# Where the expert bias is split into bf16 parts, how branch B normalises its rows, and the order of the first sums

## The chip, the cores and the metric

The kernel runs on one core of a Trainium2 chip. The metric is the time of one execution on the device in microseconds (us), median of several runs. One core has TensorE (PE in the profile; PEld is its weight load), VectorE (DVE), ScalarE (ACT), GpSimd (POOL) and SyncE (SP, which here only issues DMAs and waits). Every engine runs its own list of instructions in order, and they meet at semaphores.

## The reference

One decoder layer on 512 tokens of width 1024. Cut to what matters here:

```python
h = rms_norm(x, g_mix_pre) * (1.0 + sc_m) + sh_m           # sc, sh, gt: six parts of silu(c) @ w_ada + b_ada
qa, ka, va, qb, kb, vb, gza, gzb = split(h @ w_in)
o_a = sliding_window_attention(qa, ka, va, sinks, bias_a)  # branch A, 8 heads
# branch B, 4 heads with two softmaxes each, in blocks of 128 queries:
sc = jnp.einsum('bhmqd,bhmkd->bhmqk', qblk, kt)            # m = 0, 1
p = jax.nn.softmax(where(dist >= 0, sc + bias, -inf), axis=-1)
a = p[:, :, 0] - lam * p[:, :, 1]
o = einsum('bhqk,bhkd->bqhd', a, vt)
o_b = rms_norm(o, subln_g, 1e-5) * (1.0 - lam_init)
y = sigmoid(gza) * (o_a @ w_out[:512]) + sigmoid(gzb) * (o_b @ w_out[512:])
x = x + gt_m * rms_norm(y, g_mix_post)
h = rms_norm(x, g_ffn_pre) * (1.0 + sc_f) + sh_f
# 32 experts, top 4 of them for a token, blocks of 128 rows of one expert:
gu = xb @ w_gate_up[e] + b_gate_up[e]                      # up is used as clip(up) + 1
yb = clamped_swiglu(gu) @ w_down[e] + b_down[e]
```

## The kernel before

Weights and activations are fp32. In the projection and in the experts each is split into a high part (a rounding copy, on ACT) and a low part (original minus high, on DVE), and three matmuls with the parts stand for one (`three`, lines 1610 to 1612).

Stage 1, the modulation (0 to 48 us of the trace). The row silu(c) @ w_ada is made in halves of 512 contracted rows (`FIRST_MODS`, numbered 0 to 7). Halves 1, 3 and 7 are done by PE (`row_half`, L1557), the others by DVE as four multiply-adds each (`first_ada`, L1707 and L1709) whose result PE sums over partitions (`row_sum`, L1563). Between them DVE scales the four blocks of the input x (`hx`, L1736), PE transposes each (L1592) and ACT copies it out (`ht`, L1468). `hx` has two buffers, so DVE's third block waits for PE's first transposes. ACT copies finished rows (`mrow`, L1476), PE turns them to columns (`columns`, L1570), and with the last of these DVE forms the columns `shcol` and `gcol` (L1752, L1753), applies them to `ht` (L1762) and makes the high and low parts `hh` and `hl` that the projection multiplies. The first weight half of the projection is split in between: high part on ACT (L1480) after the four row copies, low part on DVE (L1745) after its first sums.

Stage 2, the projection (48 to 249 us): after K and V of branch A, eight units `u` of 512 columns (N_T = 3 transposed ones to `qk`, then five to `nat`). A unit is two weight halves, 48 matmuls each. ACT splits the second half when the unit before is done (`acc_done`), the first half of the next unit when this unit's first half is used (`half0_used`), and copies out the four sums of the unit (L1509). DVE makes the low parts and, between them, the later modulation sums (`ada`, L1724). POOL in this time issues DMAs only: small inputs, `oh` and, later, the table of position biases (`toep`), by way of DRAM.

Stage 3, attention (249 to 369 us): 24 units `UNITS`, for each block n = 0 to 3 of 128 queries two units of branch A (4 heads each) and four units of branch B (one head each, both softmaxes, keys 0 to n). PE's order is transposed(i), scores(i+3), values(i). DVE's is, in step i: after(i+1), which divides the exponentials by their sums, and before(i+3), which adds bias and takes the maximum; after the last B unit of a block `sub_norm` (L553 and L558, with a power on POOL in between, L1812). ACT's is copies(i), which brings the transposed probabilities to SBUF (L606), and exps(i+3) (L590), which also sums the rows. In steps 8 to 14 DVE does in addition one of seven `bias_parts` each (L538 to L549): they split the experts' gate and up bias `ball` (loaded three times, 32 rows each) into three bf16 parts `bparts` of 96 rows in all, which later a matmul adds to each expert's sums.

Stage 4, merge, router and tables (369 to about 480 us), and stage 5, the experts (to the end), aren't touched but for one wait of PE at their head.

For a unit of B, after(i) is four instructions: two reciprocals in one (L524), the second times minus lambda (L526), the first probabilities times the first reciprocal (L527), and the sum of both (L529).

## Time and profile before

| | |
|---|---|
| median of 3 runs | 1775.54 us (1775.3 to 1778.35) |
| the profiled execution | 1777.53 us, of which the span of the trace is 1775.7 us |
| PE busy | 1663.3 us, 94% of the span |
| DVE busy | 1377.4 us, 78% |
| ACT busy | 1097.6 us, 62% |
| POOL busy | 199.0 us, 11% |
| mean granted TensorE clock | 0.953 of full |

A share over the whole span is mostly that of the experts, which take two thirds of it; the stages before them have other limits, so the views are to be read by stage. A timeline row is: start in us, duration, engine, line, operation, output <- inputs, count of merged instructions, and in brackets the idle time before it with what ended it. The granted clock is 1.00 at 2.4 GHz and 0.50 at 1.2 GHz; a value in between is a mean over a stretch with both.

### The profile page before, as it was taken

Reading aid. Unit: us, or ns where it says so; the run is one execution under the profiler, and the core shown is the slowest. Engines: PE = TensorE matmul, PEld = TensorE weight load, DVE = VectorE, ACT = ScalarE, POOL = GpSimd, SP = SyncE. Lnnn points to the kernel's source line nnn. Section 1 sums busy time; section 2 is a strip of 40 time slices with the busy share of each in tenths; the row PEclk is TensorE's granted clock in tenths of the full one; section 3 lists DMA queues with packets and bytes.
Section 4 is the critical chain, followed back from the end, with each engine's and each line's share of the span. In section 5 each row is a group of like instructions: output and inputs, shape, how many; then the busy total and the mean of one; then the engine's idle time right before and its main releaser. Section 6 shows DMA issues by size and latency. Waiting matters only on the chain.

```text
span 1775.7 us, 19642 instructions
## 1 busy us (share of the span) xinstructions
PE 1663.3 (94%) x7482; PEld 1299.8 (73%) x7482; DVE 1377.4 (78%) x1029; ACT 1097.6 (62%) x903; POOL 199.0 (11%) x154
## 2 busy tenths in 40 slices
PE   8999986688679999999999999999999999999994
PEld 3788864444368888888888888888888888888882
DVE  3544458825558888988898889988989898989894
ACT  2322235531447777777777777777777777777772
POOL 1200000021300001100110011001000100011112
PEclk9999997888579999999999999999999999999997
DMA  8765430022499999999999999999999999999964
GB/s 310 226 236 198 168 125 1 1 77 73 140 361 398 390 385 381 367 386 382 378 355 388 383 375 366 388 392 380 361 383 387 375 370 390 380 370 361 382 244 155
DMA packets 156502, 540.14 MB, mean 304 GB/s; under 512 B 13949, under 2 KB 15081, under 8 KB 156292
## 3 DMA queue, kind: packets, MB, share of 16 engines
q1 hardware_dynamic: 140880, 500.20, 74.0%
q0 software_dynamic: 13424, 34.47, 8.0%
q10 hardware_dynamic: 2100, 4.21, 0.7%
q8 instruction: 57, 0.93, 0.2%
q14 instruction: 41, 0.33, 0.0%
HBM read 522.54 MB, written 29.26 MB: 311 GB/s over the span
## 4 chain that ended last, share of the span: by engine, by line
PE 74%; DMA 2%; DVE 2%; ACT 1%; issue 1%; POOL 0%; POOLq 0%; SPq 0%; ACTq 0%; DVEq 0%
PE ps L1103 64%; PE ps L1077 4%; PE ps L651 4%; PE ps L1093 2%; PE ps L671 1%; DMA expert_sums<-yb,icur 0%; DMA xb<-h_ffn,stab 0%; DMA sums<-expert_sums 0%; PE ps L449 0%; PE ps L664 0%; ACT h2t L755 0%; DMA slot_rows<-rows,dest 0%; DVE y L831 0%; DVE yo L1364 0%; POOL slot_rows L931 0%
## 5 line engine op out<-in xcount | busy, mean ns | idle before, releaser
L1221 DVE TENSOR_TENSOR wl<-rawm,wh 128x2048 fp32r<-128x2048 f32 x420 | 946.7, 2286 | 147.6 <-ACT wh L1150 143.1
L1150 ACT ACTIVATE wh<-rawm 128x2048 fp32r<-128x2048 f32 x420 | 802.0, 1919 | 260.7 <-PE ps L1103 260.7
L1103 PE MATMUL ps<-wh,xh 128*128 128x512 f32 x1120 | 360.2, 403 | 3.5 <-DVE xl L1234 3.5
L1103 PE MATMUL ps<-wl,xh 128*128 128x512 f32 x1120 | 346.9, 391 | 0.0
L1103 PE MATMUL ps<-wh,xl 128*128 128x512 f32 x1120 | 346.2, 390 | 0.0
L1103 PEld LDWEIGHTS ps<-wh,xh 128*128 128x128 f32 x1120 | 211.3, 189 | 53.1 <-DVE xl L1234 4.9
L1103 PEld LDWEIGHTS ps<-wl,xh 128*128 128x128 f32 x1120 | 211.2, 189 | 44.8
L1103 PEld LDWEIGHTS ps<-wh,xl 128*128 128x128 f32 x1120 | 211.3, 189 | 44.5
L1103 PE MATMUL ps<-wh,ah 128*128 128x512 f32 x560 | 179.4, 401 | 2.5 <-DVE al L1238 2.5
L1103 PE MATMUL ps<-wl,ah 128*128 128x512 f32 x560 | 174.2, 392 | 0.0
L1103 PE MATMUL ps<-wh,al 128*128 128x512 f32 x560 | 173.1, 390 | 0.0
L1306 POOL DMA_INDIRECT expert_sums<-yb,stab x32 | 50.9, 1590 | 1009.0 <-ACT yb L1184 658.1
L1103 PEld LDWEIGHTS ps<-wh,al 128*128 128x128 f32 x560 | 105.6, 189 | 23.1
L1103 PEld LDWEIGHTS ps<-wl,ah 128*128 128x128 f32 x560 | 105.5, 188 | 22.7
L1103 PEld LDWEIGHTS ps<-wh,ah 128*128 128x128 f32 x560 | 100.3, 189 | 19.6 <-issue 3.0
L1745 DVE TENSOR_TENSOR wlf<-raw,whf 128x2048 fp32r<-128x2048 f32 (+1 forms) x18 | 39.1, 2173 | 90.1 <-ACT whf L1480 90.1
L1480 ACT ACTIVATE whf<-raw 128x2048 fp32r<-128x2048 f32 (+1 forms) x18 | 32.7, 1817 | 64.2 <-PE ps L1612 64.0
L1610 PE MATMUL ps<-whf,hh 128*128 128x512 f32 (+1 forms) x192 | 71.3, 372 | 0.0
L1612 PE MATMUL ps<-whf,hl 128*128 128x512 f32 (+1 forms) x192 | 71.1, 370 | 0.0
L1611 PE MATMUL ps<-wlf,hh 128*128 128x512 f32 (+1 forms) x192 | 71.0, 370 | 0.0
L1295 POOL DMA_INDIRECT xb<-h_ffn,stab x32 | 65.4, 2043 | 47.5 <-PE ps L1077 36.1
L1176 ACT ACTIVATE ah<-ps 128x1024 fp32r<-128x1024 f32 x35 | 35.9, 1026 | 55.3 <-PE ps L1103 55.3
(254 smaller groups left out, 1610.5 us busy)
## 6 DMA issues: line engine op xcount, KB each, us to landing
rawm<-in_w_gate_up SPq DMA_DIRECT2D x280, 1024.0 KB, 9.6
rawm<-in_w_down SPq DMA_DIRECT2D x140, 1024.0 KB, 7.8
raw<-in_w_ada SPq DMA_DIRECT2D x20, 1024.0 KB, 5.1
raw<-in_w_in SPq DMA_DIRECT2D x16, 1024.0 KB, 5.2
rawx<-in_w_ada SPq DMA_DIRECT2D x4, 1024.0 KB, 15.5
wo<-in_w_out SPq DMA_DIRECT2D x2, 2048.0 KB, 15.6
bias_vectors_repeated<-bias_vectors POOLq DMA_DIRECT2D x1, 2304.0 KB, 15.6
xs<-in_x ACTq DMA_DIRECT2D x1, 2048.0 KB, 12.9
```

Of the source, the lines that this page charges most:

```text
L651: ins = nc.tensor.matmul(ps[:, 2 * b + half, :], src[:, k, t * P:(t + 1) * P], wo[:, 4 * b + k, half * UN:(half + 1) * UN], start=(k == 0) ...
L1077: ins = nc.tensor.transpose(TURNED[:, k // 4, (k % 4) * P:(k % 4 + 1) * P], src[:, k * P:(k + 1) * P], ident[:])
L1103: ins = nc.tensor.matmul(banks[:, n, :], left[:, kk, :], right[:, k, n * UN:(n + 1) * UN], start=begins and kk == 0 and i == 0, stop=kk == ...
L1150: nc.scalar.activation(flat(wh[v % SPL][:]), flat(rawm[v][:]), ACT.Copy).then_inc(wh_done, 1)
L1176: nc.scalar.activation(flat(ah[:]), flat(TURNED), ACT.Copy).then_inc(ah_done, 1)
L1221: nc.vector.tensor_tensor(flat(wl[v][:]), flat(rawm[v][:]), flat(wh[v % SPL][:]), ALU.subtract).then_inc(wl_done, 1)
L1295: pool.indirect_dma_start(out=xb[:], out_offset=None, in_=h2_d, in_offset=bass.IndirectOffsetOnAxis(ap=column(0, p, gcur, p - (E - 1)), ax ...
L1306: pool.indirect_dma_start(out=sum_d, out_offset=bass.IndirectOffsetOnAxis(ap=column(1, p, done, p - (E - 1) if done is scur else 1), axis= ...
L1610: nc.tensor.matmul(dst, a_h, b_h, start=first, stop=False)
L1611: nc.tensor.matmul(dst, a_h, b_l, start=False, stop=False)
L1612: return nc.tensor.matmul(dst, a_l, b_h, start=False, stop=last)
L1745: nc.vector.tensor_tensor(wlf[:, m_slot, :, 0:n], raw[:, slot, :, 0:n], whf[:, m_slot, :, 0:n], ALU.subtract).then_inc(raw_used, 1)
```

## The change

Three things.

1. `ball` moves to other memory (124 KB, where `ht` lies until `hl` is made), is loaded by POOL after `hl`, and its seven parts are made by DVE in the projection's first three units, into `bmade` (132 KB). POOL writes `bmade` to DRAM behind the toep loads, and reads it back to `bparts` at the head of attention. ACT waits for the write before it begins the first unit that writes `nat`, which overlies both; PE waits for the read at the head of the merge.
2. In branch B the first probabilities are no longer divided by their sum s. The row is s times what it was, so the second factor is multiplied by s, and the row norm, which takes out any factor of a row, has its epsilon multiplied by s squared (`beps`). The sums go to `bsum`, one for each head, with two buffers over blocks.
3. `first_ada(4)`, the fifth half, is summed by DVE between the second and the third input block instead of after the fourth; ACT splits the first weight half's high part ahead of the third row copy instead of after the fourth.

```diff
--- before.py
+++ after.py
@@ -108,6 +108,7 @@
     wide_d = dram("bias_vectors_repeated", (H_A + H_B, P, REL), F32)
     x1_d = dram("x_after_mixing", (T, D), F32)
     h2_d = dram("h_ffn", (T, D), F32)
+    bparts_d = dram("gate_up_bias_parts", (96, 2 * D), BF16)
     slot_d = dram("slot_rows", (T * E, 2), I32)
     sum_d = dram("expert_sums", (T + P, D), F32)
 
@@ -132,7 +133,8 @@
     otb = at("otb", [P, H_B, T], F32, 24 * KB)
     on = at("on", [P, H_B, P], F32, 32 * KB)
     osq = at("osq", [P, P], F32, 34 * KB)
-    ball = at("ball", [96, 2 * D], F32, 52 * KB)
+    ball = at("ball", [96, 2 * D], F32, 124 * KB)
+    bmade = at("bmade", [96, 2 * D], BF16, 132 * KB)
     wo = at("wo", [P, KC, D], F32, 64 * KB)
 
     y1 = at("y1", [P, 2, D], F32, 0)
@@ -241,6 +243,8 @@
     st = at("st", [P, IN_FLIGHT, 8, 4], F32, 35 * KB)
     NMX, MX, DSK, ESK, SUM, DEN, FAC = range(7)
     sn = at("sn", [P, 3, H_B], F32, 35 * KB + 512)
+    bsum = at("bsum", [P, 2, H_B], F32, 35 * KB + 576)
+    beps = at("beps", [P, H_B], F32, 35 * KB + 608)
 
 
     r_at = [166 * KB]
...
@@ -365,7 +369,7 @@
         return 5 if u[0] == "A" else 2
 
     def n_den(u):
-        return 2 if u[0] == "A" else 3
+        return 2
 
     def n_a(i):
         return sum(u[0] == "A" for u in UNITS[:i + 1])
@@ -521,38 +525,23 @@
                 nc.vector.tensor_tensor(dst, dst, st[:, w, FAC, :].unsqueeze(2).to_broadcast([P, 4, width]),
                                         ALU.mult).then_inc(p_ready, 1)
                 return
-            nc.vector.reciprocal(st[:, w, FAC, 0:2], st[:, w, SUM, 0:2]).then_inc(den_step, 1)
-            dve.wait_ge(den_step, total(n_den, i) - 2)
-            nc.vector.tensor_tensor(st[:, w, DEN, 0:1], st[:, w, FAC, 1:2], nlam[:], ALU.mult).then_inc(den_step, 1)
-            nc.vector.tensor_scalar(dst[:, 0, :], dst[:, 0, :], st[:, w, FAC, 0:1], None, ALU.mult).then_inc(den_step, 1)
+            nc.vector.reciprocal(st[:, w, FAC, 1:2], st[:, w, SUM, 1:2]).then_inc(den_step, 1)
+            dve.wait_ge(den_step, total(n_den, i) - 1)
+            nc.vector.scalar_tensor_tensor(st[:, w, DEN, 0:1], st[:, w, FAC, 1:2], nlam[:, 0:1], bsum[:, n % 2, g:g + 1],
+                                           ALU.mult, ALU.mult).then_inc(den_step, 1)
             dve.wait_ge(den_step, total(n_den, i))
             nc.vector.scalar_tensor_tensor(dst[:, 0, :], dst[:, 1, :], st[:, w, DEN, 0:1], dst[:, 0, :], ALU.mult,
                                            ALU.add).then_inc(p_ready, 1)
 
-        def bias_parts(n):
-
-
-            if n == 0:
-                dve.wait_ge(ball_in, 16 * 3)
-                dve.wait_ge(latemod_ready, 3)
-                nc.vector.tensor_scalar(ball[:, D:2 * D], ball[:, D:2 * D], 1.0, None, ALU.add).then_inc(bias_step, 1)
-                dve.wait_ge(bias_step, 1)
-                nc.vector.tensor_copy(bparts[:], ball[:]).then_inc(bias_step, 1)
-                return
-
-            cut, lo = ((False, 1), (False, 2), (True, 1), (True, 2), (False, 2), (True, 2))[n - 1]
-            rows = slice(32 * lo, 32 * lo + 32)
-            dve.wait_ge(bias_step, n + 1)
-            if cut:
-                nc.vector.tensor_copy(bparts[rows, :], ball[rows, :]).then_inc(bias_step, 1)
-            else:
-                nc.vector.tensor_tensor(ball[rows, :], ball[rows, :], bparts[rows, :], ALU.subtract).then_inc(bias_step, 1)
-
         def sub_norm(n):
+
+            nc.vector.scalar_tensor_tensor(beps[:], bsum[:, n % 2, :], EPS_SUB, bsum[:, n % 2, :], ALU.mult,
+                                           ALU.mult).then_inc(sn_ready, 1)
+            dve.wait_ge(sn_ready, 3 * n + 1)
             dve.wait_ge(osq_ready, H_B * (n + 1))
-            nc.vector.tensor_scalar(sn[:, 1, :], sn[:, 0, :], 1.0 / (2 * DH), EPS_SUB, ALU.mult,
-                                    ALU.add).then_inc(sn_ready, 1)
-            dve.wait_ge(sn_ready, 2 * n + 2)
+            nc.vector.scalar_tensor_tensor(sn[:, 1, :], sn[:, 0, :], 1.0 / (2 * DH), beps[:], ALU.mult,
+                                           ALU.add).then_inc(sn_ready, 1)
+            dve.wait_ge(sn_ready, 3 * n + 3)
             if n:
                 dve.wait_ge(ot_ps, n)
             nc.vector.tensor_tensor(on[:], ps[:, 7, :].rearrange("p (h d) -> p h d", h=H_B),
@@ -576,8 +565,6 @@
                 before(i + AHEAD)
             if i and UNITS[i - 1][0] == "B" and UNITS[i - 1][2] == H_B - 1:
                 sub_norm(UNITS[i - 1][1])
-            if 8 <= i < 8 + N_BIAS:
-                bias_parts(i - 8)
         sub_norm(TC - 1)
 
     def attention_act(act):
@@ -586,9 +573,12 @@
             w = i % IN_FLIGHT
             dst = scores_sb(i)
             act.wait_ge(mx_step, total(n_max, i))
+            if kind == "B" and n >= 2:
+                act.wait_ge(on_ready, n - 1)
             for m in range(dst.shape[1]):
+                sums_to = bsum[:, n % 2, g:g + 1] if kind == "B" and m == 0 else st[:, w, SUM, m:m + 1]
                 nc.scalar.activation(dst[:, m, :], dst[:, m, :], ACT.Exp, bias=st[:, w, NMX, m:m + 1],
-                                     accum_out=st[:, w, SUM, m:m + 1]).then_inc(exp_ready, 1)
+                                     accum_out=sums_to).then_inc(exp_ready, 1)
             if kind == "A":
                 nc.scalar.activation(st[:, w, ESK, :], st[:, w, DSK, :], ACT.Exp).then_inc(exp_ready, 1)
 
@@ -632,11 +622,12 @@
 
     def attention_pool(pool, power):
         for n in range(TC):
-            power(sn[:, 2, :], sn[:, 1, :], sn_ready, 2 * n + 1)
+            power(sn[:, 2, :], sn[:, 1, :], sn_ready, 3 * n + 2)
 
 
     def merge_pe(pe):
         pe.wait_ge(wo_in, 32)
+        pe.wait_ge(bias_moved, 16 * 5)
 
         def branches(t):
             pe.wait_ge(o_ready, 2 * (t + 1))
@@ -1468,18 +1459,19 @@
             nc.scalar.activation(ht[:, :, t * P:(t + 1) * P], ps[:, b:b + 2, :].rearrange("p a (b c) -> p (a b) c", c=P),
                                  ACT.Copy).then_inc(ht_copied, 1)
 
+        def split_high(m, slot, m_slot, arrivals, n=UN):
+            act.wait_ge(raw_in[slot], 16 * arrivals)
+            nc.scalar.activation(whf[:, m_slot, :, 0:n], raw[:, slot, :, 0:n], ACT.Copy).then_inc(wh_ready, 1)
+
         for n, j in enumerate((0, 2, 1, 3)):
+            if n == 2:
+                split_high(0, 0, 0, 2, 256)
             if n:
                 act.wait_ge(row_ps, n)
             else:
                 act.wait_ge(pe_ada, 2)
             nc.scalar.activation(mrow[:, j, :], ps[0:1, j, :], ACT.Copy).then_inc(mrow_ready, 1)
 
-        def split_high(m, slot, m_slot, arrivals, n=UN):
-            act.wait_ge(raw_in[slot], 16 * arrivals)
-            nc.scalar.activation(whf[:, m_slot, :, 0:n], raw[:, slot, :, 0:n], ACT.Copy).then_inc(wh_ready, 1)
-
-        split_high(0, 0, 0, 2, 256)
 
         for k in range(KC):
             act.wait_ge(h_ready, k + 1)
@@ -1516,6 +1508,7 @@
 
         with act.Fori(0, N_T) as u:
             unit(u, to_qk)
+        act.wait_ge(bias_moved, 16 * 4)
         with act.Fori(N_T, N_W - 1) as u:
             unit(u, to_nat)
 
@@ -1734,8 +1727,9 @@
             if t >= 2:
                 dve.wait_ge(ht_ps, t - 1)
             nc.vector.tensor_scalar(hx[:, t % 2, :], xs[:, t, :], rs[:, 2, t:t + 1], None, ALU.mult).then_inc(hx_ready, 1)
-
-        first_ada(4, 6, None)
+            if t == 1:
+                first_ada(4, 6, None)
+
         first_ada(5, 9, None)
         first_ada(6, 12, 3)
 
@@ -1787,7 +1781,28 @@
             else:
                 ada(4 + u, 1, 1, 3 + u, 13 + 4 * u, 12 + 4 * u)
 
-        with dve.Fori(0, N_W - 1) as u:
+        def bias_parts(n):
+
+            if n == 0:
+                dve.wait_ge(bias_moved, 16 * 3)
+                nc.vector.tensor_scalar(ball[:, D:2 * D], ball[:, D:2 * D], 1.0, None, ALU.add).then_inc(bias_step, 1)
+                dve.wait_ge(bias_step, 1)
+                nc.vector.tensor_copy(bmade[:], ball[:]).then_inc(bias_step, 1)
+                return
+
+            cut, lo = ((False, 1), (False, 2), (True, 1), (True, 2), (False, 2), (True, 2))[n - 1]
+            rows = slice(32 * lo, 32 * lo + 32)
+            dve.wait_ge(bias_step, n + 1)
+            if cut:
+                nc.vector.tensor_copy(bmade[rows, :], ball[rows, :]).then_inc(bias_step, 1)
+            else:
+                nc.vector.tensor_tensor(ball[rows, :], ball[rows, :], bmade[rows, :], ALU.subtract).then_inc(bias_step, 1)
+
+        for u, parts in enumerate(((0, 1), (2, 3, 4), (5, 6))):
+            unit(u)
+            for n in parts:
+                bias_parts(n)
+        with dve.Fori(N_T, N_W - 1) as u:
             unit(u)
         dve.wait_ge(grow_in, 32)
         dve.wait_ge(latemod_ps, 1)
@@ -1831,6 +1846,9 @@
         pool.dma_start(grow2[:], bcast(g_ffn_pre[0], D)).then_inc(grow_in, 16)
         pool.wait_ge(hx_ready, TC)
         pool.dma_start(oh[:], oh_c).then_inc(oh_in, 16)
+        pool.wait_ge(hl_ready, KC)
+        for b in range(3):
+            pool.dma_start(ball[32 * b:32 * b + 32, :], b_gate_up[0]).then_inc(bias_moved, 16)
         pool.wait_ge(rv_ready, 2)
         pool.dma_start(bias_d[0:H_A, :], rv[:, 0, :]).then_inc(biasv_out, 16)
         pool.dma_start(bias_d[H_A:H_A + H_B, :], rv[0:H_B, 1, :]).then_inc(biasv_out, 16)
@@ -1850,11 +1868,14 @@
                 pool.dma_start(toep[:, 4 * g + 2 * a:4 * g + 2 * a + 2, :],
                                shifted(4 * g + a, 2, 2)).then_inc(toep_in, 16)
         pool.dma_start(toep[:, H_A:H_A + H_B, :], shifted(H_A, 1, H_B)).then_inc(toep_in, 16)
+        pool.wait_ge(bias_step, N_BIAS + 1)
+        pool.dma_start(bparts_d, bmade[:]).then_inc(bias_moved, 16)
 
         pool.wait_ge(acc_done, 5 + 4 * N_W)
         pool.dma_start(grow3[:], bcast(g_ffn_post[0], D)).then_inc(grow_in, 16)
-        for b in range(3):
-            pool.dma_start(ball[32 * b:32 * b + 32, :], b_gate_up[0]).then_inc(ball_in, 16)
+        pool.wait_ge(latemod_ready, 3)
+        pool.wait_ge(bias_moved, 16 * 4)
+        pool.dma_start(bparts[:], bparts_d).then_inc(bias_moved, 16)
         attention_pool(pool, power)
         merge_pool(pool, power)
         experts_pool(pool)
```

## Rows read from the trace of the kernel before

**Rows 1.** Busy time by stretch: stretch, length, engines, PEclk, DMA share, GB/s.
```profile
70.00:240.00 170.00, 170.00 (x745) 139.44 (x743) 81.33 (x80) 44.69 (x44) 4.82 (x6) 1.00 0.55 190
...
287.90:335.80 47.90, 31.42 (x148) 20.37 (x144) 43.94 (x76) 21.81 (x76) 1.01 (x1) 0.68 0.00 1
325.00:357.00 32.00, 22.46 (x124) 15.47 (x125) 27.91 (x56) 17.25 (x54) 1.01 (x1) 0.82 0.00 1
```

**Rows 2.** The same view of instructions on `ball` alone: stretch, length, DVE, POOL.
```profile
287.90:335.80 47.90, 12.37 (x8) 0.00 (x0) 0.68 0.00 1
```

**Rows 3.** Waits, 250 to 370 us: who waited for whom, us, times, longest.
```profile
DVE s_sb L498 <- PE ps L406: 5.8, 6, 1.6
```

**Rows 4.** DVE's timeline in attention.
```profile
302.25 0.16 DVE L517 TENSOR_TENSOR st<-st 128x4 f32<-128x4 f32 x1
...
303.80 0.68 DVE L498 SCALAR_TENSOR_TENSOR s_sb<-ps,toep 128x512 f32<-128x512 f32 x1
...
306.10 1.22 DVE L547 CAST bparts<-ball 32x2048 bf16<-32x2048 f32 x1
...
325.20 0.16 DVE L526 TENSOR_TENSOR st<-st,nlam 128x1 f32<-128x1 f32 x1
325.27 0.41 DVE L527 TENSOR_SCALAR s_sb<-s_sb,st 128x384 f32<-128x384 f32 x1
...
335.82 0.69 DVE L498 SCALAR_TENSOR_TENSOR s_sb<-ps,toep 128x512 f32<-128x512 f32 x1 [1.13 <-PE ps L406]
```

**Rows 5.** Timelines of ACT (first row) and PE in attention: one loop.
```profile
300.00 0.51 ACT L590 ACTIVATE s_sb<-s_sb,st 128x256 f32<-128x256 f32 x1 [3.83 <-DVE st L492]
302.49 1.22 PE L449 MATMUL ps<-nat,pt 128*128 128x128 f32 x4 [3.03 <-ACT pt L606]
303.94 1.97 PE L420 MATMUL ps<-ident,s_sb 128*128 128x128 f32 x8 [0.23 <-DVE s_sb L521]
305.83 1.65 PE L406 MATMUL ps<-qk 64*128 64x384 f32 x4
...
280.15 1.10 PE L420 MATMUL ps<-ident,s_sb 128*128 128x128 f32 x8
```

**Rows 6.** Timelines of DVE (three rows), PE (three), DVE (one) in stage 1.
```profile
24.91 1.63 DVE L1736 TENSOR_SCALAR hx<-xs,rs 128x1024 f32<-128x1024 f32 x2 [2.05 <-PE ps L1592]
26.46 0.48 DVE L1707 TENSOR_SCALAR acc<-rawx,cact 128x512 f32<-128x512 f32 x1
29.22 0.48 DVE L1707 TENSOR_SCALAR acc<-rawx,cact 128x512 f32<-128x512 f32 x1
27.99 1.02 PE L1563 MATMUL ps<-acc,one 128*1 128x512 f32 x2
32.11 1.87 PE L1563 MATMUL ps<-acc,one 128*1 128x512 f32 x2 [3.10 <-DVE acc L1709]
42.64 1.94 PE L1570 MATMUL ps<-one,mrow 1*128 1x1 f32 x16
45.45 0.16 DVE L1752 COPY shcol<-ps 128x8 f32<-128x8 f32 x1
```

**Rows 7.** SP's timeline, DMA issues (KB, us to landing), PE's timeline: first arrivals.
```profile
3.21 15.60 SPq L1419 DMA_DIRECT2D rawx<-in_w_ada  x4
rawx<-in_w_ada SPq DMA_DIRECT2D x1, 1024.0 KB, 19.6
oh<-const_buckets POOLq DMA_DIRECT2D x1, 99.0 KB, 14.4
66.35 0.81 PE L1639 MATMUL ps<-oh,tabx 33*8 33x384 f32 x2
```

**Rows 8.** Timelines of DVE, then ACT, around the projection's unit 3.
```profile
135.91 2.29 DVE L1745 TENSOR_TENSOR wlf<-raw,whf 128x2048 fp32r<-128x2048 f32 x1 [6.06 <-ACT whf L1480]
144.34 1.92 ACT L1480 ACTIVATE whf<-raw 128x2048 fp32r<-128x2048 f32 x1 [8.46 <-PE ps L1612]
```

**Rows 9.** DMA issues by line, 0 to 120 us: the nearest to the new write.
```profile
toep<-bias_vectors_repeated POOLq DMA_DIRECT2D x4, 256.0 KB, 6.0
```

## What the change is predicted to do

> **What bounds the kernel now.** I read the busy time by stretch first, since the page's shares are those of the experts. In the projection PE is busy for all of 170 us out of 170, at full clock, while DVE is busy for half of them and ACT for a quarter [rows 1]: whatever PE starts earlier there stays earlier, and DVE has room. In the middle of attention it is the other way round: in the 47.9 us from the end of step 8's `before` to the start of step 17's, DVE is busy 43.9 us, PE 31.4 at a mean clock of 0.68, ACT 21.8 [rows 1]. The same view for instructions on `ball` alone gives 12.4 us of DVE in it [rows 2]. That is the largest piece that the change moves, and it moves from where DVE is the bound to where PE is. The waits then say what is second: over all of attention DVE waits six times for PE's scores, 5.8 us in sum [rows 3], and those six lie outside the stretch with the bias parts or at its very end (the wait at 335.82 [rows 4]). So PE and ACT stand close behind DVE, and part of what DVE gives up is theirs. Stage 1 is a chain: DVE's sums, PE's row sums and columns, DVE's `shcol`, then the first projection matmul.
>
> **The bias parts leave attention.** From DVE's 47.9 us go 12.4 us of instructions and about 0.3 of the gaps between seven of them. The wait of 1.1 us for PE at the end [rows 4] isn't DVE's work; without it 34.1 remain.
>
> **Branch B's factor.** L527 goes. It took 0.41 us in the trace's unit of 384 keys, but it began 0.07 us after L526 [rows 4]; now L526's successor has to wait for L526 to end, some 0.1 us. Net 0.3 for 384 keys; for 128 to 512 keys 0.2 to 0.4. Six B units lie in the stretch: 1.8 us. `beps` is one more small instruction and one more wait on DVE in `sub_norm`: 0.2. DVE's own need for the stretch is then 34.1 - 1.8 + 0.2 = 32.5, that is 15.4 us less than 47.9. That is the upper bound.
>
> **What PE and ACT take back.** `before(j+2)` needs its scores, and PE makes them after a loop that starts with `before(j)`: ACT's exponentials of j, its copy, PE's values, transposes, scores. One such loop from the rows: exponentials from 300.00, values at 302.49, transposes at 303.94, scores 305.83 to 307.5: 7.5 us from `before(13)` [rows 5]. DVE's work in the same interval without a bias part: an `after` of A (302.25 to 303.80, 1.55), `before(14)` (303.80 to 306.07, 2.3), another `after` of A, 1.55: 5.4 us [rows 4]. So 2.1 us come back. But those PE pieces ran at the low clock: the eight transposes took 1.97 where the same eight took 1.10 earlier [rows 5]. With PE's 5.0 us scaled by that ratio (0.56) the loop is 5.3 us, and nothing comes back. I took the same sum for the nine intervals of the stretch: at full clock 0.8 us come back (15.4 - 0.8 = 14.6 gained), at the low one 6.5 (8.9 gained). In the neighbouring stretch, which has one bias part in it only at its edge, the clock is 0.82 [rows 1], so 0.36 of the time low: 0.8 + 0.36 x 5.7 = 2.9 back. I take 12.5 us gained, bounds 8.9 and 14.6. The other ten B units save 2.8 us of DVE, next to the six waits for PE; where DVE already waits it gains nothing, so I take 0.5 (0 to 2.8). After the last `before`, at the tail of attention, PE and ACT alone set the time: 0 there.
>
> **The rule on the clock.** The trace shows it fall when PE had stood still: the row sum after a wait of 3.1 us takes 1.87 us where the one before took 1.02 [rows 6]. The Trainium skill, page "TensorE: Matmul & The Clock Gate", section "What's actually happening", says that the throttled clock is the default and activity releases it. By that rule alone, with the bias parts' long stalls of PE gone, the stretch would run at the upper of the two bounds; the mean of 0.82 next door says that attention's normal stalls are already enough to lose it at times.
>
> **The fifth half and the first weight half.** DVE stands idle for 2.05 us between input blocks 2 and 3, waiting for PE; half 4 takes 26.46 to 29.22, 2.76 us [rows 6]. Its data was issued at 3.21 and landed 19.6 us later, at 22.8 [rows 7]; the gap begins at 22.86. So the half runs 22.9 to 25.6, the third block starts 0.7 later than now, the fourth ends 0.7 later, and half 5 starts at 27.2 instead of 29.22. PE's row sum at 32.11 waits for it and starts at 30.1: 2.0 us earlier, and all behind it with it (the last half on PE started at 35.70 behind other PE work; its data, issued some 13 us after that of half 4, is there by about 31.5, before the 33.7 at which it would now start). The third block's transposes get 0.4 later, which ends in ACT's copies and isn't late for 30.1. At the end PE's columns stop at 44.6 (42.64 + 1.94) while `shcol` starts at 45.45, since ACT's high part and DVE's low part of the first weight half came just before it [rows 6]; both now run long before, which is 0.8. Sum 2.8 us. If PE's shorter wait (0.9 for 3.1 us) also keeps the clock, the 12.5 us of PE between 32.1 and 44.6 shrink by up to 3.0 more: 5.8. No row shows whether; I take the middle, 4.3. The later row copy isn't delayed by the split: its data lands about 33, the copy is due at 38.8.
>
> **What could be late behind that.** PE needs `oh` at 66.35; it was issued at 51.1 and took 14.4 us, so it landed at 65.5 [rows 7]. Its issue is released by the columns, 20.9 us before; the matmuls before L1639 take as long from there, now that the 0.8 is gone. Margin about nothing: 0.3 us lost (0 to 1). The three `ball` loads stand behind it in POOL's queue, so they cost it nothing; who waits behind them is `rv` out and `toep`, wanted 150 us later.
>
> **The bias parts in the projection.** 4.2, 4.7 and 3.5 us at the ends of units 0, 1, 2. DVE idles for 6.1 us there before the next low part [rows 8], so they fit: 0. The wait that is added is ACT's, before unit 3, with ACT's split of the second half and DVE's low part queued behind it. DVE's sums of unit 2 end at 129.85 (135.91 less its idle 6.06), parts 5 and 6 at 133.4, POOL's write goes out at once. Nearest row: 256 KB in 6.0 us [rows 9]; this is 384 KB. Taken as 6: 139.5, ACT 141.4, DVE 143.8; PE wants it when its first half is used, at 144.34 [rows 8]. So the slack is 6.5 us after the issue, and I take 0, with up to 1.5 for a landing of 8. The read back at the head of attention has 100 us.
>
> **The sum.** 12.5 + 0.5 + 4.3 - 0.3 = 17.0 us. The profiled execution took 1777.5 us (span 1775.7), so 1760.5 for it; the median of the runs is 2.0 us lower, so the median to be expected is 1775.5 - 17.0 = 1758.5. Everything behind attention only shifts. A change of 0.2% is 3.6 us, about what a measurement here can tell from none.
>
> **Rivals.** (A) PE and ACT are the bound at the low clock: attention gains 8.9, stage 1 only 2.8 less 0.3: 1775.5 - 11.9 = 1763.6 (with the 0.5). For it: 0.68 in this very stretch. Against: PE stood still there because of the bias parts. (B) The clock stays up in both places: 14.6 + 0.5 + 5.8 - 0.3 = 20.6, 1754.9; to 1753 if the other B units give more. (C) The write of the parts lands late: each us beyond 6.5 stops PE in the projection, where it is the bound. `oh`'s 14.4 us [rows 7], the longest landing of a small POOL transfer, would stop PE 7.9 us: 1766.4, and a stop that long would also drop its clock, so some 1769. (D) The other side: the same wait, with a landing of over 6.5 + 17 = 23.5 us; at 30 us it is 1782. It decides only if POOL's queue holds the write back, for instance because the toep loads before it aren't issued yet; in the trace they are out by 90.8, so I see nothing for it. (E) Part of it does not act: half 4's data isn't there at 22.9 and DVE blocks on it with the third input block queued behind; every us late is a us of the 2.0 lost: at most 1761.
>
> **Chances.** Forecast (1756 to 1761.5) 0.55, A 0.2, B 0.13, C 0.06, E 0.04, D 0.02. The range reaches to B's 1753 and past A, to 1767 at C's edge: about 0.85. Faster by over 0.2% (below 1772): 0.96; within: 0.02; slower: 0.02.
>
> **What would show it.** Right: no bias instruction among DVE's in attention; the stretch from `before(11)` to `before(20)` 33 to 39 us long, with new waits of DVE for PE's scores of together 1 to 6 us; `shcol` at 39.7 to 42.7; the projection's PE without a gap; ACT's first split of unit 3 later by some us with no wait of PE behind it. Wrong: a wait of PE at L1639 or in unit 3, or a granted clock in the stretch that stays at 0.68.

## The result, and the profile after

| | before | after |
|---|---|---|
| time, median of 6 runs in turn, us | 1776.55 (1775.3 to 1780.97) | 1758.11 (1755.18 to 1759.54) |
| ratio, with its 95% interval | | 0.989 (0.9876 to 0.9904) |
| profiled execution, us (span) | 1777.53 (1775.7) | 1757.6 (1755.7) |
| granted clock, mean | 0.953 | 0.962 |
| busy share PE / DVE / ACT | see the table of before | 94% / 78% / 63% |

The changed kernel is 18.4 us faster (median against median), against 17.0 forecast (1758.5). One number on the whole kernel says nothing on the steps, so I took five marks from DVE's timeline in every trace: the start of `shcol`, of step 0's `before`, the end of step 11's, the start of step 20's, the start of the last `on` (the last instruction of the normalised rows of branch B). All later tables go by the lengths between them:

| us (granted clock in the last three) | before | after | moved | forecast |
|---|---|---|---|---|
| stage 1, to `shcol` | 45.45 | 39.45 | -6.0 | -4.3 (2.8 to 5.8) |
| projection, to `before(0)` | 204.37 | 204.44 | +0.1 | +0.3 |
| attention, part 1: to the end of `before(11)` | 38.12 (0.82) | 41.45 (0.71) | **+3.3** | -0.5 |
| attention, the stretch: to `before(20)` | 47.88 (0.68) | 34.76 (0.90) | -13.1 | -12.5 (8.9 to 14.6) |
| attention, tail: to the last `on` | 31.73 (0.77) | 29.93 (0.94) | -1.8 | 0 |
| the rest of the span | 1408.15 | 1405.67 | -2.5 | 0 |

Up to the last `on` the gain is 17.5 us. The rest has the same instructions in both and is between 1404.9 and 1409.1 us in all fourteen traces of this case, so its 2.5 us are scatter; between the second traces of the two kernels it is 1.5 us longer in the changed one. A nearly exact total thus hides four terms that were off: three came out better, and one had the wrong sign.

The busy time by stretch of the changed kernel (stretch, length, PE, PEld, DVE, ACT, POOL, granted clock, DMA share, GB/s): projection, part 1, the stretch, the tail.

```profile
70.00:240.00 170.00, 170.00 (x744) 139.24 (x743) 89.50 (x83) 46.28 (x47) 4.21 (x7) 1.00 0.55 187
243.89:285.34 41.45, 27.14 (x157) 18.91 (x155) 30.00 (x77) 21.43 (x86) 1.56 (x2) 0.71 0.26 100
285.34:320.10 34.76, 23.20 (x148) 15.38 (x144) 29.94 (x62) 20.53 (x71) 1.01 (x1) 0.90 0.00 1
320.10:350.03 29.93, 17.76 (x118) 13.34 (x118) 17.73 (x37) 15.29 (x47) 2.04 (x3) 0.94 0.10 36
```

The same view of the kernel before, between the same marks:

```profile
249.82:287.94 38.12, 23.35 (x157) 16.14 (x155) 30.62 (x82) 21.31 (x86) 1.05 (x1) 0.82 0.37 121
287.94:335.82 47.88, 31.38 (x148) 20.33 (x144) 43.90 (x76) 21.81 (x76) 1.01 (x1) 0.68 0.00 1
335.82:367.55 31.73, 20.84 (x118) 15.54 (x118) 18.80 (x38) 14.34 (x41) 2.05 (x3) 0.77 0.09 34
```

Three things are to be seen. The projection took DVE's bias work (89.5 us busy against 81.3 [rows 1]) and PE stayed busy for 170.00 of 170 us. In the stretch DVE lost 14.0 us of 43.9, the clock rose from 0.68 to 0.90, and PE's 148 matmuls took 23.2 us where they had taken 31.4. In part 1 the same 157 matmuls, with DVE's work slightly less, took 27.1 us where they had taken 23.4, at a lower clock.

DVE's waits in the whole of attention of the changed kernel (who waited for whom, us, times, longest), against 5.8 us in six waits at the first line before [rows 3]:

```profile
DVE s_sb L502 <- PE ps L410: 10.2, 9, 1.8
DVE sn L542 <- ACT osq L605: 6.8, 1, 6.8
```

The larger part of these waits for PE's scores lies in part 1, not in the stretch, where they are 2.4 us. DVE's waits in part 1, before (two rows) and after (two):

```profile
DVE s_sb L498 <- PE ps L406: 4.4, 4, 1.6
DVE s_sb L484 <- PE ps L401: 1.5, 2, 1.2
DVE s_sb L502 <- PE ps L410: 6.5, 5, 1.6
DVE s_sb L488 <- PE ps L405: 2.9, 2, 1.7
```

That is 5.9 us before and 9.4 after: the 3.3 us that part 1 got longer stand in DVE's waits for PE.

Stage 1: timelines of DVE, then PE. Half 4's sums now begin at 23.04, ahead of the third input block (25.81), the row sum runs 2.1 us earlier and at 1.02 us instead of 1.87, and the low part of the first weight half no longer stands right before `shcol` [rows 6].

```profile
23.04 0.49 DVE L1700 TENSOR_SCALAR acc<-rawx,cact 128x512 f32<-128x512 f32 x1
25.81 1.41 DVE L1729 TENSOR_SCALAR hx<-xs,rs 128x1024 f32<-128x1024 f32 x2
27.13 0.48 DVE L1700 TENSOR_SCALAR acc<-rawx,cact 128x512 f32<-128x512 f32 x1
34.22 1.23 DVE L1739 TENSOR_TENSOR wlf<-raw,whf 128x1024 fp32r<-128x1024 f32 x1 [1.22 <-ACT whf L1464]
39.45 0.17 DVE L1746 COPY shcol<-ps 128x8 f32<-128x8 f32 x1 [4.01 <-PE ps L1563]
28.51 1.02 PE L1556 MATMUL ps<-acc,one 128*1 128x512 f32 x2
30.03 1.02 PE L1556 MATMUL ps<-acc,one 128*1 128x512 f32 x2 [0.50 <-DVE acc L1702]
```

The projection's unit 3: DVE, POOL, ACT, DVE, ACT.

```profile
126.27 1.22 DVE L1797 CAST bmade<-ball 32x2048 bf16<-32x2048 f32 x1
127.78 0.55 POOL L1872 DMA_DIRECT2D gate_up_bias_parts<-bmade  x1 [39.94 <-DVE bmade L1797]
131.85 1.92 ACT L1464 ACTIVATE whf<-raw 128x2048 fp32r<-128x2048 f32 x1 [3.71 <-DMA gate_up_bias_parts<-bmade]
133.80 2.29 DVE L1739 TENSOR_TENSOR wlf<-raw,whf 128x2048 fp32r<-128x2048 f32 x1 [6.31 <-ACT whf L1464]
138.41 1.92 ACT L1464 ACTIVATE whf<-raw 128x2048 fp32r<-128x2048 f32 x1 [4.64 <-PE ps L1605]
```

ACT waits 3.71 us for the write, as the prediction said it would, and PE doesn't wait behind it.

### The profile page after: what moved, and what is told of

Same layout as the page of the kernel before. It is cut to its first block, busy times and chain, and to the rows that moved or that the text cites. A ratio compares the mean times of both kernels' runs of the same rounds, so it can differ in the third digit from the quotient of the medians.

```text
span 1755.7 us, 19607 instructions
## 1 busy us (share of the span) xinstructions
PE 1651.8 (94%) x7482; PEld 1294.2 (74%) x7482; DVE 1374.1 (78%) x1017; ACT 1097.7 (63%) x903; POOL 200.1 (11%) x156
## 4 chain that ended last, share of the span: by engine, by line
PE 75%; DVE 2%; DMA 2%; ACT 1%; issue 1%; POOL 0%; POOLq 0%; SPq 0%; ACTq 0%; DVEq 0%
PE ps L1094 65%; PE ps L1068 4%; PE ps L642 3%; PE ps L1084 2%; PE ps L662 1%; DMA expert_sums<-yb,icur 0%; DMA xb<-h_ffn,stab 0%; DMA sums<-expert_sums 0%; PE ps L655 0%; ACT h2t L746 0%; DMA slot_rows<-rows,dest 0%; DVE y L822 0%; PE ps L453 0%; POOL slot_rows L922 0%; DVE yo L1355 0%
## 6 DMA issues: line engine op xcount, KB each, us to landing
wo<-in_w_out SPq DMA_DIRECT2D x2, 2048.0 KB, 12.5
xs<-in_x ACTq DMA_DIRECT2D x1, 2048.0 KB, 13.1
```

## The experiments

Three questions were open: what each part is worth alone, whether the clock is really the cause in stage 1, and where part 1's 3.3 us come from. All the ratios below are to the kernel before, run in the same session. The stage lengths come from one trace of each kernel, the ratios from all its executions.

### The parts, one at a time

The new order of the first sums alone, change 3 (`first_only`; `half_only` has only the first of its two edits):

```diff
# DVE, in the loop over the input blocks (and removed behind it)
+            if t == 1:
+                first_ada(4, 6, None)
# ACT, in the loop over the row copies (and removed behind it); first_only alone
+            if n == 2:
+                split_high(0, 0, 0, 2, 256)
```

> The kernel before with the third part alone: half 4 summed between the input blocks, the first weight half's high part before the third row copy. Theory 1 (PE's shorter stop keeps its clock, and the projection carries the gain whole): shcol starts at 39.4 to 39.7 instead of 45.45, the row sum that took 1.87 us takes 1.02, the time falls by 5.9 us against the kernel before. Rival (the order alone counts, the clock was luck): shcol at 42.6, 2.8 us less. Second rival: the 5.9 us are there at the head of attention but are lost in it again, the end 3 us earlier or less.

> The kernel before with half 4 summed between the input blocks; the first weight half is split where it was. Theory 1: 2.0 us from the order and 3.0 from the clock, so shcol at 40.3 to 40.6; the 0.8 of the split is still paid. Rival (the whole of stage 1 hangs on the split's place): shcol at 44 or later.

The row factor alone, put into the kernel before:

```diff
-            nc.vector.tensor_tensor(st[:, w, DEN, 0:1], st[:, w, FAC, 1:2], nlam[:], ALU.mult)
-            nc.vector.tensor_scalar(dst[:, 0, :], dst[:, 0, :], st[:, w, FAC, 0:1], None, ALU.mult)
+            nc.vector.scalar_tensor_tensor(st[:, w, DEN, 0:1], st[:, w, FAC, 1:2], nlam[:, 0:1],
+                                           bsum[:, n % 2, g:g + 1], ALU.mult, ALU.mult)
...
+            nc.vector.scalar_tensor_tensor(beps[:], bsum[:, n % 2, :], EPS_SUB, bsum[:, n % 2, :], ...)
```

> The kernel before with branch B's first sum kept as a row factor, and nothing else. Theory 1 (DVE is the bound between the befores of units 11 and 20, and only there): the six B units in that stretch give 0.3 us each, beps costs 0.2, so 1.6 us, with 0 to 2 more from the other ten: 2 us less in all, 1 to 4. Rival (DVE's time is hidden beside PE and ACT even there): 0, within 0.5 us of the kernel before.

The bias parts alone, that is the changed kernel with both edits above taken back:

```diff
-            if t == 1:
-                first_ada(4, 6, None)
...
-            nc.vector.scalar_tensor_tensor(st[:, w, DEN, 0:1], ..., bsum[:, n % 2, g:g + 1], ...)
+            nc.vector.tensor_scalar(dst[:, 0, :], dst[:, 0, :], st[:, w, FAC, 0:1], None, ALU.mult)
```

> The kernel before with the bias parts moved to the projection, and nothing else. Theory 1 (12.7 us leave a stretch bound by DVE, PE and ACT take about 2 back at a clock of about 0.9): the stretch from the end of before(11) to the start of before(20) falls from 47.9 to about 37, the time by 10 to 12 us. Rival (PE and ACT bind at the low clock): the stretch stays at 40 or more, the time falls by 7 or less. If the wait of ACT in the projection cost anything, the head of attention would come later than in the kernel before.

And a second trace of the changed kernel with nothing edited:

> The changed kernel as it is, for a second trace and more times. In its first trace the first part of attention, from the start of before(0) to the end of before(11), took 41.4 us against 38.1 before, though DVE has less to do in it. Theory 1 (the phase in which PE's clock falls and rises, which differs between executions): this trace gives 37 to 42 and another clock in it than 0.65. Rival (something in the change makes it longer, such as the extra DMA or the new waits): 41 to 42 again with the same stalls. The time is 17 to 19 us less than the kernel before.

| us (clock) | stage 1 | projection | part 1 | stretch | tail | median, ratio (interval) |
|---|---|---|---|---|---|---|
| before | 45.45 | 204.37 | 38.12 (0.82) | 47.88 (0.68) | 31.73 (0.77) | |
| first_only | 39.32 | 204.62 | 41.84 (0.67) | 47.79 (0.68) | 30.70 (0.83) | 1771.62, 0.9957 (0.9942 to 0.9972) |
| half_only | 40.08 | 204.62 | 41.86 (0.67) | 47.83 (0.68) | 30.78 (0.83) | 1773.81, 0.9975 (0.9963 to 0.9988) |
| factor_only | 45.26 | 204.27 | 41.30 (0.71) | 47.28 (0.68) | 28.14 (0.99) | 1777.22, 0.9982 (0.9971 to 0.9993) |
| bias_only | 45.90 | 207.81 | 38.22 (0.82) | 35.25 (0.90) | 29.91 (0.94) | 1770.31, 0.9949 (0.9934 to 0.9964) |
| after_again | 39.28 | 204.81 | 41.42 (0.63) | 34.46 (0.90) | 30.23 (0.94) | 1760.24, 0.9889 (0.9871 to 0.9906) |

By their ratios the parts are worth 7.6, 3.2 and 9.1 us, together 19.9, against 19.8 for the whole kernel in that session. Each of these is known to some 2 to 3 us only. By the marks of their traces they win 3.3, 1.3 and 10.5 us up to the last `on`, together 15.0, against 17.5 for the whole. What each is worth is not what the prediction gave it, though.

`first_only` wins 6.1 us in stage 1 and in its trace gives 3.7 back in part 1, in which it has not one instruction that differs. Its ratio (7.6 us, 5.0 to 10.3) doesn't show that loss; more on this below. `half_only` against it shows the split of the first weight half: 0.76 us (forecast 0.8).

`factor_only` was to win in the stretch and hardly does: 0.6 us, where the six B units were to give 1.8. DVE is busy 42.60 us in it instead of 43.90; of these 1.3 us about half, 0.7, went into its wait for PE's scores at the stretch's end (1.80 us instead of 1.13 [rows 4]). Its 3.6 us in the tail, at a clock of 0.99, are more than its whole gain, and it too loses 3.2 us in part 1. The edit itself costs what was forecast. In the changed kernel's B unit the multiplication starts 0.45 us after the reciprocal, where before it was 0.72 (325.00 to 325.72), so 0.27 are saved for 384 keys (forecast 0.3). The changed kernel's rows:

```profile
314.80 0.16 DVE L528 RECIPROCAL st<-st 128x1 f32<-128x1 f32 x1
314.99 0.22 DVE L530 SCALAR_TENSOR_TENSOR st<-st,nlam,bsum 128x1 f32<-128x1 f32 x1
315.25 0.62 DVE L533 SCALAR_TENSOR_TENSOR s_sb<-s_sb,st 128x384 f32<-128x384 f32 x1
```

With the bias parts gone as well it brings no more: the stretch is 35.25 us in `bias_only` and 34.76 in the changed kernel, 0.5 less.

`bias_only` wins 12.6 us in the stretch and 1.8 in the tail, and loses 3.4 in the projection. Its PE timeline in the projection, and the clock behind the wait in it (view by stretch):

```profile
68.65 0.80 PE L1624 MATMUL ps<-oh,tabx 33*8 33x384 f32 x2 [1.69 <-DMA oh<-const_buckets]
70.00:80.00 10.00, 10.00 (x38) 8.11 (x38) 6.32 (x11) 0.00 (x0) 2.16 (x3) 0.83 1.00 308
```

PE waited 1.69 us for `oh`, and then ran 10 us at 0.83, where before and after it is at 1.00 there: 1.7 more. That is the 3.4.

### `oh` and the loads behind it

The prediction said that the three `ball` loads stand behind `oh` in POOL's queue and so cost it nothing. To test it they were moved behind `rv` and `toep`:

```diff
         pool.dma_start(oh[:], oh_c).then_inc(oh_in, 16)
-        pool.wait_ge(hl_ready, KC)
-        for b in range(3):
-            pool.dma_start(ball[32 * b:32 * b + 32, :], b_gate_up[0]).then_inc(bias_moved, 16)
...
         pool.wait_ge(biasv_out, 32)
+        pool.wait_ge(hl_ready, KC)
+        for b in range(3):
+            pool.dma_start(ball[32 * b:32 * b + 32, :], b_gate_up[0]).then_inc(bias_moved, 16)
```

> The move of the bias parts alone, with the three loads of the bias issued after PE has used oh, behind the first write of the position biases, instead of right behind hl. In the move alone as it was, oh took 17.0 us to land instead of 14.4, PE waited 1.7 us for it and the projection took 207.8 us instead of 204.4. Theory 1 (the loads share the DMA engines with oh though they are behind it in POOL's queue): oh lands within 15 us, no wait, projection 204.4, time 3 us below that of the move alone. Rival (something else made oh late): the wait is there again. Third: the position biases, now behind the loads, come too late for attention: DVE would wait at its head.

The issue of `oh` to its landing (KB, us), in the kernels before, first_only, after, bias_only, bias_only_load_later:

```profile
oh<-const_buckets POOLq DMA_DIRECT2D x1, 99.0 KB, 14.4
oh<-const_buckets POOLq DMA_DIRECT2D x1, 99.0 KB, 12.1
oh<-const_buckets POOLq DMA_DIRECT2D x1, 99.0 KB, 14.2
oh<-const_buckets POOLq DMA_DIRECT2D x1, 99.0 KB, 17.0
oh<-const_buckets POOLq DMA_DIRECT2D x1, 99.0 KB, 14.6
```

With the loads behind it the landing takes 2.1 us more with the timing of the new order (12.1 to 14.2) and 2.6 more with the old one (14.4 to 17.0); with the loads later it is 14.6 again, and the projection 204.95 instead of 207.81. So a transfer that is issued later in the same queue does slow the one ahead of it here. The other traces agree. Without the loads `oh` took 12.1 us in `first_only` and 14.4 to 15.0 in the five others. With both edits of `first_only` in place it took 13.9 to 14.7 with the loads right behind it (five traces) and 12.4 with the loads later (`fill_all_load_later` below). The changed kernel gets by not because `oh` starts earlier (its issue moved by 5.1 us, from 51.09 to 46.00, and PE's need of it by 5.9, from 66.35 to 60.4) but because its landing without the loads would be some 12.1 us: PE didn't wait in one trace and waited 0.45 us in the other. Why the landing is shorter with the split moved too (`first_only`) than without (`half_only`, 14.8) wasn't looked into.

In the time the gain isn't shown: the ratio is 0.9939 (0.9924 to 0.9954) against 0.9949, 1.8 us less, and the intervals overlap. Nor can the two traces be set against each other as a whole: that of `bias_only` (1767.16) is the fastest of its six executions, that of `bias_only_load_later` (1769.21, with 41.91 us in part 1) the slowest of its six.

### The write of the parts

```diff
         pool.wait_ge(bias_step, N_BIAS + 1)
+        pool.dma_start(spare_d, bmade[:]).then_inc(spare_out, 16)
+        pool.wait_ge(spare_out, 16)
+        pool.dma_start(spare_d, bmade[:]).then_inc(spare_out, 16)
+        pool.wait_ge(spare_out, 32)
         pool.dma_start(bparts_d, bmade[:]).then_inc(bias_moved, 16)
```

> The changed kernel with two more writes of the parts to another place in DRAM, one after the other, ahead of the one that ACT waits for. In the trace one write takes about 4 us from issue to the end of ACT's wait, and PE has 2.3 us left after DVE's low part. Theory 1 (each us beyond the slack stops PE in the projection): the write is there about 8 us later, PE stops for 5 to 6 us once in unit 3, with some 1 to 2 more for the clock; the projection takes 210 to 213 us instead of 204.4, the time is 6 to 8 us above the changed kernel. Rival (ACT's wait has room in the next units too, and PE catches up): less than 3.

In the changed kernel the write took 3.8 us to land (forecast 6, from a transfer of 256 KB [rows 9]). `late_write`'s waits (who for whom, us, times, longest), ACT's timeline and its clock in the stretch behind the wait:

```profile
PE ps L1605 <- DVE wlf L1741: 4.5, 1, 4.5
138.10 3.71 ACT L1466 ACTIVATE whf<-raw 128x2048 fp32r<-128x2048 f32 x2 [10.36 <-DMA gate_up_bias_parts<-bmade]
142.40:147.00 4.60, 4.60 (x11) 3.63 (x12) 4.49 (x5) 0.00 (x0) 0.00 (x0) 0.50 0.74 222
```

PE waits 4.5 us, and behind it the clock is 0.50 for at least 4.6 us, which costs 2.3 or a little more: the projection takes 211.61, 7.2 longer, and the time rises by some 6 (1763.66; 0.9924, 0.9906 to 0.9943, against 0.989 for the changed kernel). The mechanism of rival C is real and its price right; only its condition isn't met. ACT's split began 6.25 us later than in the changed kernel (138.10 against 131.85), in a projection that ran 0.4 us ahead of that kernel's until then. PE lost 4.5 of these 6.65, so some 2.2 us of slack were left there.

### The clock in stage 1

Before, PE's wait of 3.1 us is filled with three products that nobody reads, and nothing is moved:

```diff
         row_sum(2, True)
+        pe.wait_ge(ht_copied, TC - 1)
+        for _ in range(3):
+            nc.tensor.matmul(ps[0:1, 5, :], one[:, 0:1], accf[:, 2 * UN:3 * UN], start=True, stop=True)
         pe.wait_ge(dve_ada, 4)
```

> The kernel before with three added matmuls of one row, whose result nobody reads, in PE's gap between the first and the second row sum (29.0 to 32.1 us). Nothing is moved. Theory 1 (the 3.1 us stop is what lowers the clock, and the lowered clock is half of what the order brings in stage 1): the second row sum takes 1.0 us instead of 1.87 and shcol starts 2.5 to 3 us earlier, at 42.5 to 43, the time falls by about 3. Rival (the clock falls at its own times, whatever PE does in that gap): 1.87 again, shcol at 45.4 or later.

Its PE timeline; the second row is the one that started at 32.11 and took 1.87 [rows 6]:

```profile
28.75 2.74 PE L1599 MATMUL ps<-acc,one 128*1 128x512 f32 x6
32.01 1.02 PE L1563 MATMUL ps<-acc,one 128*1 128x512 f32 x2 [0.52 <-DVE acc L1712]
```

`shcol` came at 42.2 instead of 45.45. The row sum still started at 32.0, so these 3.3 us are the clock's alone (in the five traces with the old code of this stage it takes 45.3 to 46.9 us, so the size is less sure than the cause); `half_only`'s 5.4 are then 2.2 of order (its row sum starts at 29.89) and 3.2 of clock. The time fell by 2.7 (1775.92; 0.9985, 0.9974 to 0.9995), while in the trace part 1 of attention took 41.16 with a code that is that of before: 3.0 more.

### Part 1 of attention

My first theory was that such a loss belongs to the execution and not to the kernel. A second trace of the kernel before, not edited:

> The kernel before as it is, for a second trace. In the first one the part of attention from the start of before(0) to the end of before(11) took 38.1 us; in three kernels whose attention is the same code (one with added matmuls in stage 1, two with stage 1 reordered) it took 41.2 to 41.9, with PE's clock low for longer. Theory 1 (the first trace had the clock on its side there, which this code does not earn): 38 or 41 to 42, and whichever it is, the granted clock goes with it, 0.82 or about 0.7. Rival (38.1 belongs to the kernel before, and an earlier start of attention costs it 3 us): 38.1 again.

It gave 38.55 us at 0.82, the changed kernel twice 41.4, and I took the theory as fallen. By traces, part 1 takes 38.1 to 38.6 us in before, before_again and bias_only, and 41.1 to 41.9 in after, after_again, first_only, half_only, factor_only, before_pe_kept_busy, late_write and bias_only_load_later. The rival, that an attention which starts earlier pays for it, doesn't fit: factor_only starts at 249.5, beside before's 249.8, and takes 41.3; bias_only_load_later starts at 251.9, later than before, and takes 41.9. What goes with the length is the granted clock: 0.82 in the short ones, 0.63 to 0.71 in the long ones. At steps of half a us, in before it is low from 4 to 11 and from 21 to 28 us after `before(0)`; in after from 4 to 11, 14.5 to 18 and 21.5 to 35. In after_again it is low without a break from 3.5 to 34, and part 1 is no longer for it (41.42). Common to all eight long ones is that the clock is low beyond 28 us, to 33 to 35; in the three short ones it isn't.

Two traces of a kernel are few, though, and the times of the executions without a trace speak for the first theory:

- `factor_only`'s twelve executions fall into two groups: five of 1773.8 to 1774.8 us at a mean clock of 0.957, and seven of 1777.1 to 1779.7 at 0.952 to 0.954. The traced one, with 41.3 us in part 1, is of the second. The groups lie some 4 us and 0.004 apart. By an estimate from the rows, part 1's two patterns differ by 3 us, and by some 10 us of low clock (0.36 of 38.1 us against 0.58 of 41.3), which makes 0.003 in the mean clock of an execution: about the same.
- `bias_only`'s trace, with the short part 1, is the fastest of its six (1767.16 at 0.962; the others 1768.1 to 1773.1 at 0.956 to 0.960).
- Both traces of the kernel before are at 0.953 and some 1777.4 us. Of its 45 executions in the later sessions 25 are at 0.951 or lower, with a median time of 1780.1 us, and 20 above it, with 1777.3.
- The ratios of `first_only`, `half_only`, `factor_only` and `before_pe_kept_busy` give each 2 to 4 us more than their marks against before's (7.6 for 3.3, 4.4 for 2.4, 3.2 for 1.3, 2.7 for 0.3). `bias_only`, whose trace has the short part 1 as well, gives 9.1 for 10.5.

All this is as it would be if one kernel had either pattern from one execution to the next, and both traces of before happened on the short one. It isn't shown, since only a traced execution has marks; but that the pattern belongs to the kernel isn't shown either.

So the clock itself was to be moved. At the head of attention PE has its longest stop, 6.1 us, for step 0's exponentials and the division behind them. It was filled with matmuls whose result nobody reads:

```diff
         for i in range(AHEAD):
             scores(i)
+        pe.wait_ge(latemod_ready, 2)
+        for _ in range(6):
+            nc.tensor.matmul(ps[:, 5, 0:UN], ident[:], qk[:, 0, 0:UN], start=True, stop=True)
```

> The changed kernel with six added matmuls of 512 columns in PE's stop of 6.1 us at the head of attention, whose result nobody reads. Theory 1 (PE's stops there lower its clock, and the low clock makes PE's loop longer than DVE's work): the clock is not low from 4 to 11 us after before(0), the first part falls from 41.4 to 38 to 39, the time by about 3 us against the changed kernel. Rival (the later stops lower it anyway): the first part stays at 41, the time is unchanged or 1 us more.

Its view by stretch, and PE's timeline at the head:

```profile
246.21:284.71 38.50, 27.96 (x169) 18.36 (x167) 30.03 (x77) 21.41 (x86) 1.57 (x2) 0.87 0.29 110
247.38 5.42 PE L467 MATMUL ps<-qk,ident 128*128 128x512 f32 x12
253.18 0.66 PE L424 MATMUL ps<-ident,s_sb 128*128 128x128 f32 x4 [0.38 <-DVE s_sb L532]
```

Part 1 is 38.50 us at 0.87, though PE has 12 matmuls more: 2.95 less than in the changed kernel. With the two kernels below that are filled at the same place it is three short ones of three, against three of eleven without. DVE's work in it is the same (30.03 us against 30.00), and its waits for PE's scores are 6.8 us instead of 9.4. So the clock is very likely what costs the 3 us; with one trace of each kernel, chance isn't shut out. Here the clock is low from 21 to 31 us only. Gone are the low stretches from 4 to 11, which the short traces without a filling have too, and those from 14.5 to 18 and from 31 to 35. How a filled stop at 4 us changes what comes 27 us later isn't shown.

The time stayed where it was: 1757.79 (0.9881, 0.9865 to 0.9898, against 0.989). The traced execution was the slowest of its four (1760.02, the others 1755.4 to 1757.8). PE waited 1.05 us for `oh` in it, its projection took 206.35, 1.9 more, and the rest of its span 1408.8. That accounts for the trace, not for the median.

Two more on top of it: two short products in each B unit of attention as well, and then the `ball` loads moved as above. The table has the other kernels of this and the last sections too.

```diff
                 scores(i + AHEAD)
+            if UNITS[i][0] == "B":
+                filler(2, 256)
             values(i)
```

> The same with, in addition, two added matmuls of 256 columns in each unit of branch B, where PE waits for ACT's copy. Theory 1: the clock is low in less than a fifth of attention, the first part takes 37 to 38 us, the stretch from before(11) to before(20) 33 to 34.8, the time falls by 4 to 6 us against the changed kernel. Rival (PE does not always wait there; the added work of about 1 us a unit delays the real one): the part and the stretch get longer, the time is 0 to 6 us more.

> The same with, in addition, the loads of the bias issued after PE has used oh. Theory 1: oh lands in about 12 us instead of 14.2 to 14.7 and the 0 to 0.45 us that PE waited for it in the changed kernel are gone; 0 to 0.5 us less than without. Rival: the loads stand before the position biases, whose way through DRAM ends just as early as it must: DVE waits at the head of attention.

| us (clock) | stage 1 | projection | part 1 | stretch | tail | median, ratio (interval) |
|---|---|---|---|---|---|---|
| fill_head | 39.86 | 206.35 | 38.50 (0.87) | 34.43 (0.90) | 30.26 (0.94) | 1757.79, 0.9881 (0.9865 to 0.9898) |
| fill_all | 39.3 | 204.91 | 38.91 (0.87) | 34.75 (0.95) | 30.2 (0.94) | 1757.39, 0.9881 (0.9865 to 0.9898) |
| fill_all_load_later | 39.4 | 204.28 | 38.55 (0.87) | 34.22 (1.00) | 30.08 (0.94) | 1754.69, 0.9874 (0.9858 to 0.9891) |
| before_again | 45.55 | 204.78 | 38.55 (0.82) | 47.79 (0.68) | 31.76 (0.77) | 1777.36, one execution |
| before_pe_kept_busy | 42.20 | 204.17 | 41.16 (0.71) | 47.92 (0.68) | 31.76 (0.77) | 1775.92, 0.9985 (0.9974 to 0.9995) |
| bias_only_load_later | 46.90 | 204.95 | 41.91 (0.67) | 35.29 (0.90) | 29.88 (0.94) | 1768.49, 0.9939 (0.9924 to 0.9954) |
| late_write | 39.40 | 211.61 | 41.12 (0.67) | 33.85 (0.95) | 29.90 (0.94) | 1763.66, 0.9924 (0.9906 to 0.9943) |

The products in the B units bring nothing: the stretch is 34.2 to 34.8 us at 0.90, 0.95 and 1.00 alike, and in `late_write`, without any products, 33.85 at 0.95. At full clock at most some 0.5 us are left to win there; what sets it then, DVE (29.87 us busy) or the order of the steps, wasn't separated. The last kernel ends attention at 346.5 instead of 350.0 and has the lowest median of all, but its interval overlaps the changed kernel's, so it isn't shown to be faster.

## Why the prediction was right, and where not

- **The stretch** (forecast 12.5, measured 13.1 and, between the second traces, 13.3). DVE's work came out nearly as worked out: the bias parts took 12.7 us with them (bias_only's 31.23 against 43.90; forecast 12.4 and 0.3 of gaps), the factor 1.3 (29.94 against 31.23; forecast 1.6). DVE's own need was put at 32.5 us and the stretch took 34.76, so PE and ACT took back 2.3 us, where I had put 2.9 from the neighbouring clock of 0.82; DVE's waits for PE's scores in it are 2.4. The clock was 0.90. At 1.00 (fill_all_load_later) the stretch took 34.22 us and at 0.95 (late_write) 33.85, so that my upper bound of 14.6 was 0.6 to 0.9 too high even there. The rule of the Trainium skill (page "TensorE: Matmul & The Clock Gate", section "What's actually happening"), activity releases the clock, leans the right way: PE's waits for the copied probabilities fell from 14.7 us to 10.8, and the clock rose from 0.68 to 0.90.
- **The tail** (forecast 0, measured 1.8 and 1.5). The step "after the last `before` PE and ACT alone set the time: 0 there" holds, but I read the zero from the work and forgot that PE's pace there is the clock's: 0.77 to 0.94, PE's 118 matmuls from 20.8 to 17.8 us. `bias_only`, whose code there is that of before, has the same 1.8 us. The same argument that I used in the stretch was due here.
- **The other ten B units** (forecast 0.5, measured +3.3 in part 1). The step assumed that what has no edit keeps its time. It failed by the clock's second pattern, which is worth 3 us in the traces and came with DVE's waits for PE, 9.4 us instead of 5.9. No row of before shows it.
- **The order in stage 1** (forecast 2.0 + 0.8, measured 2.1 to 2.2 and 0.76): right. **The clock there** (forecast half of 3.0, measured 3.3 alone): the middle was taken for want of a row; with the stop of 0.50 us that was left the clock stayed up. The clock either fell there or didn't, so the middle of the two was a value that no run could give. That made stage 1 -6.0, just past its upper bound of 5.8.
- **`oh`** (forecast 0.3; the projection took 0.1 us more, and in the second trace PE waited 0.45): the size is right and the reason is wrong. "They cost it nothing" is refuted, with 2.1 to 2.6 us; it didn't matter because the timing of the new order had brought the landing down to 12.1, which wasn't foreseen and is luck. Without that order it cost 3.4 us.
- **The write** (forecast 0): right, with a landing of 3.8 us for the 6 taken. The slack was put at 6.5 us behind the issue; ACT began 4.1 us behind it and 2.2 were left, so 6.3.
- **The sum.** 3.8 us lost in part 1 against the forecast meet 1.7 in stage 1, 1.8 in the tail, 0.6 in the stretch and 0.2 at `oh`, 4.3 in all; 17.0 becomes 17.5 up to the last `on`. The total was right in part by chance. If the traces of before happened on the shorter part 1, as the times suggest, the 3.8 belong in part to that choice of trace.

What stays open: why the clock is low for longer in part 1 of some traces and not of others. It follows neither the start of attention nor its code. The length was the same in the two traces of each kernel that has two, the clock was not (0.71 and 0.63 in the changed one), and the spread of the times suggests that it differs between executions of one kernel. A second and third trace of `factor_only`, from either of its groups, would settle it. Which of the stops decides wasn't separated.

## What to carry to other kernels

Move work from where its engine is the bound to where the engine idles beside another that is, and price what returns at the clock that the stretch will have, not at the one it has. Do that for the stretches beside it too: a stage whose PE work is cut up by stops lost or won some 2 to 3 us here with the clock, its instructions unchanged. One trace of each kernel is not enough for a stage of that kind: compare the spread of the times, and their mean clocks, with the execution that was traced. Look at what shares the queue with a small transfer that PE awaits, also behind it. And hold the result against marks per stage, since here four errors of 0.6 to 3.8 us ended as one of 0.5.

## What the runs showed of the hardware

- Length and granted clock of part 1 of attention, with nearly the same code, fell into two groups of traces: 38.1 to 38.6 us at 0.82 (three), and 41.1 to 41.9 at 0.63 to 0.71 (eight).
- In the projection a stop of PE of 1.69 us was followed by a mean clock of 0.83 from 70 to 80 us, one of 1.05 us by 0.75 from 60 to 65 (fill_head), one of 4.5 us by 4.6 us at 0.50; stops of 0.50 in stage 1 and 0.45 in the projection by no loss.
- A stop filled with one-row products or with products that nobody reads kept the clock in stage 1 (1.02 us instead of 1.87 for the same pair) and, in the first stop, at the head of attention. It delayed nothing there: the row sum began at 32.0 us instead of 32.1, the first transposes 7.0 us after `before(0)` instead of 7.4.
- 768 KB issued behind a transfer of 99 KB in the same queue made that one land 2.1 to 2.6 us later (17.0 against 14.4, 14.2 against 12.1), and issuing them later took 2.4 and 2.2 back (17.0 to 14.6, 14.6 to 12.4).
